# Rotation on VectorE a quad ahead, products of rounded activations first, roundings moved in the norm gaps, and the inverse's first turn placed earlier

## The reference, cut

```python
def _layer(x, pos, st, lp):
    h = _rmsnorm(x, lp['norm_mix_pre'])
    y, new_st = _token_mixers(h, pos, st, lp)     # 4 mLSTM, 4 retention, 8 gated-delta heads of 128
    x = x + _rmsnorm(y, lp['norm_mix_post'])
    h = _rmsnorm(x, lp['norm_mlp_pre'])
    u = jnp.square(jax.nn.relu(jnp.einsum('btd,df->btf', h, lp['w_up'])))      # 2048 -> 8192
    x = x + _rmsnorm(jnp.einsum('btf,fd->btd', u, lp['w_down']), lp['norm_mlp_post'])
    return x, new_st

def _rotary(x, pos):                              # q and k of the retention heads
    x1, x2 = x[..., :half], x[..., half:]
    return jnp.concatenate([x1 * cos - x2 * sin, x1 * sin + x2 * cos], axis=-1)
```

## Time and profile before

| | us |
|---|---|
| median of 3 runs | 3140.09 (3137.81 to 3142.33) |
| profiled execution | 3140.11 |
| its span, first to last instruction | 3138.6 |
| TensorE busy | 3054.0, 97% |
| VectorE busy | 1919.4, 61% |
| ScalarE busy | 1542.6, 49% |
| mean granted clock of TensorE | 0.994 |

### The profile page before, as it was taken

The page is one execution under the profiler, slowest core; times in us unless marked ns, Lnnn a source line. Parts: engine busy times, 40 slices in busy tenths (PEclk is TensorE's granted clock), DMA queues, the critical chain, the costliest instruction groups (busy, mean ns, idle before and its releaser), DMA issues.

```text
span 3138.6 us, 66992 instructions
## 1 busy us (share of the span) xinstructions
PE 3054.0 (97%) x23012; PEld 2985.0 (95%) x23012; DVE 1919.4 (61%) x3994; ACT 1542.6 (49%) x3580; POOL 85.6 (3%) x163
## 2 busy tenths in 40 slices
PE   8999999999999999999999999999999999999998
PEld 7999999998999999999989999999989999999997
DVE  6677776656545545455576777766565454554555
ACT  6476665545333334334455676655454333343343
POOL 1100000000000000000001000000000000000000
PEclk9999999999999999999999999999999999999999
DMA  6554445553544444444445444455535445444444
GB/s 210 178 153 138 140 140 157 168 180 127 170 165 161 165 162 167 161 162 166 155 142 177 146 145 143 138 163 159 171 129 167 160 163 167 165 162 166 163 164 155
DMA packets 267255, 499.96 MB, mean 159 GB/s; under 512 B 34528, under 2 KB 39936, under 8 KB 267072
## 3 DMA queue, kind: packets, MB, share of 16 engines
q1 hardware_dynamic: 244224, 443.64, 43.9%
q0 software_dynamic: 14784, 51.05, 4.7%
q10 hardware_dynamic: 8064, 2.80, 0.3%
HBM read 475.38 MB, written 22.01 MB: 158 GB/s over the span
## 4 chain that ended last, share of the span: by engine, by line
PE 80%; DVE 11%; ACT 5%; issue 3%; DMA 1%; ACTq 0%; DVEq 0%; POOL 0%; SPq 0%; POOLq 0%
PE PU L523 72%; PE PABCD L523 3%; DVE WL L1300 2%; PE PE_ L523 2%; PE PF L523 2%; ACT AE L899 1%; ACT Y L899 1%; DVE AE L1687 1%; ACT WH L899 1%; DMA RAW<-in_w 1%; DVE Y L1484 1%; DVE Y L1320 1%; DVE X L1327 0%; DVE HL L1305 0%; DVE AM L1592 0%
## 5 line engine op out<-in xcount | busy, mean ns | idle before, releaser
L523 PE MATMUL PU<-HH,WH 128*128 128x288 f32 x4000 | 1236.4, 309 | 29.5 <-DVE HL L1305 21.1
L899 ACT ACTIVATE WH<-RAW 128x512 fp32r<-128x512 f32 x1669 | 965.4, 621 | 583.4 <-PE PU L523 436.6
L1300 DVE TENSOR_TENSOR WL<-RAW,WH 128x512 fp32r<-128x512 f32 x1668 | 1077.1, 687 | 271.1 <-ACT WH L899 258.0
L523 PE MATMUL PU<-HL,WH 128*128 128x288 f32 x4000 | 1183.2, 296 | 0.0
L523 PE MATMUL PU<-HH,WL 128*128 128x288 f32 x4000 | 1180.2, 295 | 0.0
L523 PEld LDWEIGHTS PU<-HH,WH 128*128 128x128 f32 x4000 | 754.4, 189 | 61.1 <-issue 41.6
L523 PE MATMUL PU<-UH,WH 128*128 128x288 f32 x2560 | 759.1, 297 | 2.8 <-DVE UL L1475 1.9
L523 PEld LDWEIGHTS PU<-HL,WH 128*128 128x128 f32 x4000 | 755.9, 189 | 4.1
L523 PEld LDWEIGHTS PU<-HH,WL 128*128 128x128 f32 x4000 | 755.9, 189 | 0.0
L523 PE MATMUL PU<-UL,WH 128*128 128x288 f32 x2560 | 755.2, 295 | 0.0
L523 PE MATMUL PU<-UH,WL 128*128 128x288 f32 x2560 | 752.6, 294 | 0.0
(11 more groups left out here) (281 smaller groups left out, 2214.7 us busy)
## 6 DMA issues: line engine op xcount, KB each, us to landing
RAW<-in_w SPq DMA_DIRECT2D x1669, 256.0 KB, 3.8
SIN<-in_sin POOLq DMA_DIRECT2D x32, 512.0 KB, 4.9
out_sout<-Y POOLq DMA_DIRECT2D x32, 512.0 KB, 5.4
BC<-gate_rows POOLq DMA_DIRECT2D x32, 304.0 KB, 4.4
AUX<-in_aux POOLq DMA_DIRECT2D x32, 152.0 KB, 3.2
X<-in_x SPq DMA_DIRECT2D x4, 576.0 KB, 8.6
out_y<-X SPq DMA_DIRECT2D x8, 288.0 KB, 2.1
out_sout<-SOUT ACTq DMA_DIRECT2D x32, 64.0 KB, 2.4
```

The source lines that it names most:

```text
L523: return nc.tensor.matmul(out, lhsT, rhs, start=start, stop=stop, skip_group_check=True)
L899: return nc.scalar.activation(out, in_, f, **kw)
L1300: tt(WL[s % 2][:, k], RAW[c][:], WH[s % 2][:, k].bitcast(F32), ALU.subtract).then_inc(sem("lo_ready"), 1)
```

## The change

- **Rotation.** The two `c_rot` products and step 1's three VectorE instructions go. `rotate` does the same with four VectorE instructions in the quad ahead: z times cosine (128 rows), two halves of 64 rows of z times sine, each read from one half of the rows and written to the other, and the sum into QK2. They stand at slots 16, 17, 19 and 21 of the retention quads and at 19 to 22 of "first". Step 2 of a retention head moves from slot 8 to slot 6.
- **Order of products.** In quads with two units at once `pair_part` does, for each pair of chunks, the products with HH for both units (8 matmuls) in an even slot, waiting for `hh_ready`, and the products with HL (4 matmuls) in the odd slot behind it, waiting for `hl_ready`. Both units are done at slot 15.
- **Roundings in the gap.** `hi_part(Q, 4)` and `lo_part(Q, 4)` stand ahead of the norm's factor; pieces 5, 6 and 7 follow in groups 1, 3 and 5 on both engines. The last chunk's weighing by the gain (`weigh`) stands behind the factor.
- **Inverse.** XM is transposed at slot 3, ahead of NX, into Q2 and not XT.
- **Start.** The first gain is loaded by ScalarE's queue and not GpSimd's, and ScalarE rounds the first weights before it waits for it.

```diff
+RET_SLOTS = {**LINEAR_SLOTS, 2: 6}
+ROTATE_SLOTS, FIRST_ROTATE_SLOTS = (16, 17, 19, 21), (19, 20, 21, 22)
-SIDE_BY_SIDE = [(t % 2, t // 2) for t in range(16)] + [divmod(t, 8) for t in range(16, SLOTS)]
...
+            def pair_part(Q, t, kind, l):
+
+                kk, low = divmod(t, 2)
+                e = 2 * l + (1 if kind == "up_first" else 0)
+                if t == 0:
+                    pe.wait_ge(sem("psum_read"), 4 * Q + 2)
+                if not low and kk % 2 == 0:
+                    pe.wait_ge(sem("lo_ready"), 16 * Q + 4 + kk // 2 + 1)
+                for s in range(2):
+                    psum = PU[s][:, 0:T]
+                    for k in (2 * kk, 2 * kk + 1):
+                        if s == 0:
+                            pe.wait_ge(sem("hl_ready" if low else "hh_ready"), e * NC_ + k + 1)
+                        if low:
+                            last = mm(psum, WH[s][:, k], HL[:, k], False, k == NC_ - 1)
+                        else:
+                            mm(psum, WH[s][:, k], HH[:, k], k == 0, False)
+                            mm(psum, WL[s][:, k], HH[:, k], False, False)
+                    if t == 15:
+                        last.then_inc(sem("unit_done"), 1)
...
-                if step == 0 and not mls:
+                if step == 2:
                     pe.wait_ge(sem("z_ready"), 4 * n + 4)
-                    pe.wait_ge(sem("state_ready"), n + 1)
-                    mm(PC[:, 0:T], con["c_rot"][:], z[:, 0])
-                    mm(PD[:, 0:T], con["c_rot"][:], z[:, 1]).then_inc(sem("ret_rotated"), 1)
...
         def _(act):
+            act.dma_start(NG0[:], d["ng0"][0]).then_inc(sem("gain_at_start_in"), 16)
...
             def prenorm(l, e, gain, Q):
...
-                    if (e or l) and g in (0, 1, 3, 5):
-                        hi_part(Q, (g + 1) // 2 + 4)
+                    if (e or l) and g in (1, 3, 5):
+                        hi_part(Q, g // 2 + 5)
...
             def after_out(l):
+                Q = l * QUADS + HEADS + NC_ // 4
+                hi_part(Q, 4)
                 norm_scale(2 * l + 1, RS, "rs_ready")
-                prenorm(l, 2, NG[:, 1], l * QUADS + HEADS + NC_ // 4)
+                weigh(l, 0, NC_ - 1)
+                prenorm(l, 2, NG[:, 1], Q)
...
+            def rotate(t, nk, par, slots):
+
+                z, half = Z[par], HD // 2
+                cos, sin = con["c_cos"], con["c_sin"]
+                if t == slots[0]:
+                    dve.wait_ge(sem("constants_in"), 16 * len(con))
+                    tt(ACC[:, 0:2, 0:T], z[:, 0:2], cos[:].unsqueeze(1).to_broadcast([128, 2, T]), ALU.mult).then_inc(sem("ret_qk"), 1)
+                for j, (a, b) in ((1, (half, 0)), (2, (0, half))):
+                    if t == slots[j]:
+                        tt(EE[b:b + half, 0:2, 0:T], z[a:a + half, 0:2], sin[a:a + half].unsqueeze(1).to_broadcast([half, 2, T]), ALU.mult)\
+                            .then_inc(sem("ret_qk"), 1)
+                if t == slots[3]:
+                    dve.wait_ge(sem("ret_qk"), 4 * nk + 3)
+                    tt(QK2, ACC[:, 0:2, 0:T], EE[:, 0:2, 0:T], ALU.add).then_inc(sem("ret_qk"), 1)
...
                     dve.wait_ge(sem("gdn_root"), 2 * nk + 1)
+                    nc.vector.transpose(Q2, XM).then_inc(sem("gdn_root_turned"), 1)
                     tt(NX, EYES[:], XM, ALU.subtract).then_inc(sem("gdn_root"), 1)
...
-                if t == ROOT_SLOT:
-
-                    dve.wait_ge(sem("kv_turned"), n + 1)
-                    dve.wait_ge(sem("gdn_root"), 2 * nk + 1)
-                    nc.vector.transpose(XT, XM).then_inc(sem("gdn_root_turned"), 1)
...
             def update_and_split(l, which, lo_l, lo_which, lo_gain, Q):
 
+                lo_part(Q, 4)
                 for g in range(8):
                     scale_y(l, which, g)
                     if g != 1:
...
                     if g:
                         add_x(l, which, g)
                     if g in (1, 3, 5):
-                        lo_part(Q, g // 2 + 4)
+                        lo_part(Q, g // 2 + 5)
                 prenorm_lo(lo_l, lo_which, lo_gain, range(14, 16))
-                lo_part(Q, 7)
```

More of the change, by code:

```diff
@@ L526, in turn @@
                 return nc.tensor.transpose(out, in_, IDENT)
+            def pair_part(Q, t, kind, l):
[17 more added lines that the diff above has]
+                        last.then_inc(sem("unit_done"), 1)
             def unit_part(Q, t, kind, l, x, joined):
-                s, kk = JOINED[t] if joined else SIDE_BY_SIDE[t] if two_at_once(kind, l) else divmod(t, 8)
+                if two_at_once(kind, l) and t < 16:
+                    pair_part(Q, t, kind, l)
+                    return
+                s, kk = JOINED[t] if joined else divmod(t, 8)
                 hi, lo = (UH, UL) if kind in ("out", "down", "down0", "down_last") else (HH, HL)
@@ L644, in linear_head @@
                     pe.wait_ge(sem("head_done"), n + 1)
[L645 removed]
+                if step == 2:
                     pe.wait_ge(sem("z_ready"), 4 * n + 4)
[L647 to L654 removed]
+                    if not mls:
+                        pe.wait_ge(sem("ret_qk"), 4 * (nk + 1))
                     pe.wait_ge(sem("state_ready"), n + 1)
@@ L868, in mixer @@
                         linear_select(read_number(kind, l, x))
-                    for step, slot in (LAST_SLOTS if last else EARLY_SLOTS if early else LINEAR_SLOTS).items():
+                    for step, slot in (LAST_SLOTS if last else EARLY_SLOTS if early else RET_SLOTS if kind == "ret" else LINEAR_SLOTS).items():
                         if t == slot:
@@ L972, in output_squares, with weigh @@
                     act.wait_ge(sem("gains_in"), 16 * (l + 1))
-                gain = NG[:, 0 if kind == "out" else 2, c:c + 1]
-                fn(Y[:, c], Y[:, c], scale=gain).then_inc(sem("output_squares"), 1)
+                if c < NC_ - 1:
+                    weigh(l, 0 if kind == "out" else 2, c)
+            def weigh(l, which, c):
+                fn(Y[:, c], Y[:, c], scale=NG[:, which, c:c + 1]).then_inc(sem("output_squares"), 1)
             def norm_scale(count, dst, name):
@@ L1501, in linear_head @@
                             ts(CUR[:, :, j:j + 1], COLA[:, :, bass.ds(hk + r, 1)], 1.0, None, ALU.mult).then_inc(sem("mls_cur"), 1)
-                if step == 1 and not mls:
-                    tt(ACC[:, 0:2, 0:T], z[:, 0:2], con["c_cos"][:].unsqueeze(1).to_broadcast([128, 2, T]), ALU.mult)\
-                        .then_inc(sem("ret_qk"), 1)
-                    dve.wait_ge(sem("ret_rotated"), nk + 1)
-                    tt(EE[:, 0:2, 0:T], PABCD[:, 2:4, 0:T], con["c_sin"][:].unsqueeze(1).to_broadcast([128, 2, T]), ALU.mult)\
-                        .then_inc(sem("ret_qk"), 1)
-                    dve.wait_ge(sem("ret_qk"), 3 * nk + 2)
-                    tt(QK2, ACC[:, 0:2, 0:T], EE[:, 0:2, 0:T], ALU.add).then_inc(sem("ret_qk"), 1)
                 if step == 1 and mls:
@@ L1798, in quad @@
                         lo_part(Q, t // 2 + 4, l if last_head else None)
+                    if kind == "first":
+                        rotate(t, l * H_B, 0, FIRST_ROTATE_SLOTS)
+                    if kind == "ret" and not front:
+                        rotate(t, x[1] + 1, 1 - x[3], ROTATE_SLOTS)
                     if front:
```

34 lines of the change are left out of this document (17 added, 17 removed).

## The result

The changed kernel takes **3154.2 us** (median of 5 runs, 3153.0 to 3156.8) where the kernel before takes 3141.0 beside it: ratio **1.0044**, 95% interval 1.0033 to 1.0055, so 10 to 17 us slower. The forecast was 3145.1 us with a range up to 3154. The profiled span is 3153.6 us against 3138.6, which is 15.0 us more; the mean granted clock is 0.994 in both.

The account below looks back on a forecast made before the run. TensorE, busy 97% of the span, was taken as the bound, through its work and waits. 3140.1 - 8.8 (inverse) - 5.5 (rotation) + 19.3 (gaps with clock) = 3145.1 us, start 0; range 3134 to 3154 us.

Parts of the forecast that it names:

- The norm gaps: Three gaps with two units at once: VectorE's low parts stand for ScalarE's roundings, unit 2 loses cover; 16.9 us more.
- The clock: Ends of the norm gaps: one more stretch at half clock in one gap of three, 2.4 us more.
- Rival 1: Norm gaps' ends: waits bring the clock down at each, 7 us and not 2.4; 3150 us, chance 0.20.
- The inverse's turn: Delta heads: TensorE's wait at slot 6 goes, part returns at slot 7; 0.55 us a head, 8.8 us less.
- The rotation: Retention heads: two fp32 products leave TensorE in each of 8; 4.9 us gained, heads 0 lose 0.3 each; 5.5 us less.
- The start: Kernel start: ScalarE's earlier first rounding is lost again at the next; 0, ends 0.9 us gained and 0.4 us lost.
- The sum's second term: The rotation's gain in the retention heads, 5.5 us subtracted in the sum.
- the gaps at their upper end: Norm gaps, clock included: 19.3 us more was forecast, with ends 15 and 24.

Follow-up runs that it names:

- gap_early: The changed kernel with ScalarE rounding pieces 5, 6 and 7 in groups 0, 2 and 4 of the norm gaps, not 1, 3 and 5: 3134.0 us.
- old_order: As gap_early, but TensorE takes the products of two units at once in the order of the kernel before: 3130.8 us.
- rot_only: The kernel before with the rotation's part of the change alone (VectorE, quad ahead; step 2 in slot 6): 3146.2 us, ratio 1.0012.
- turn_only: The kernel before with only the inverse's transpose moved ahead of NX, its result into Q2: 3131.7 us, ratio 0.9968.
- gw_later: The changed kernel with GpSimd holding the gates' weights' two loads until the second quarter of X has landed: 3152.2 us, one execution.
- gap_state: As gap_early, with GpSimd holding the first head's states' load until the gates' reciprocal, not only the gates' projection: 3131.4 us.
- first_thin: The changed kernel with the first quads' four rotation instructions taking 32 of their 288 columns: 3153.2 us, ratio 1.0033.

## Why the prediction was wrong, step by step

**The norm gaps: right.** Three low parts stand 2.22 us each (2.35 foretold), and unit 2 has its wait of 1.31 us (1.4 foretold). The three gaps cost 5.7, 5.9 and 6.0 us (4.7, 6.6 and 5.6 foretold), together 17.6 us (16.9 foretold without the clock, 19.3 with it). gap_early shows that they hang on the stalls, and old_order that the lost cover costs more than the shorter tail gives.

**The clock: mis-sized.** I added 2.4 us for a stretch of half clock that the kernel before would not have had. Windows (columns as in the earlier trace rows) of the changed kernel at the end of its first gap, in layer 1's MLP gap and in the first retention head of layer 1, then of the kernel before and of rot_only in layer 1's MLP gap:

```profile
752.00:755.40 3.40, 3.40 (x16) 3.25 (x14) 1.47 (x3) 1.63 (x4) 0.00 (x0) 0.51 0.00 0
2314.00:2330.00 16.00, 11.08 (x69) 7.83 (x70) 10.65 (x21) 8.66 (x21) 0.00 (x0) 1.00 0.10 34
1629.10:1632.50 3.40, 3.40 (x16) 3.22 (x15) 0.92 (x4) 1.96 (x6) 0.00 (x0) 0.50 0.48 154
```
```profile
2314.00:2320.00 6.00, 6.00 (x43) 5.69 (x43) 3.97 (x7) 4.46 (x10) 0.00 (x0) 1.00 0.49 167
```
```profile
2314.00:2320.00 6.00, 5.25 (x30) 4.18 (x31) 1.61 (x4) 2.02 (x5) 0.00 (x0) 0.72 0.13 44
```

So the changed kernel ends its first gap at the 1.2 GHz level, as the kernel before did, and the last one at 2.4 GHz, again as before; in the first quad of layer 1 each of them has one such stretch. Rival 1 did not happen: the gaps' ends have no such stretch more than before, and of the 2.4 us nothing came. What one such stretch at a gap's end costs is seen in rot_only, whose gap is the old code: unit 2 starts 26.56 us behind the first scaling instead of 25.18, 1.4 us. The changed kernel has its extra one where I had none, in the first retention head of layer 1, right behind TensorE's wait of 1.87 us for the spread at 1628.79; the kernel before has no low stretch in its retention quads. It is a likely part of the +0.9 us there (layer 0: -0.2), and in gap_early the same head of layer 0 has one (from 57.9, behind a wait of 2.10 us).
The section that the prediction cites from the Trainium skill ("TensorE: Matmul & The Clock Gate", HAM oscillation) describes a kernel in which every burst of products starts low behind a wait for a transfer; those waits were longer than the ones here, and I carried the rule over without that. Here the traces have both, with the same code: behind equal waits in layer 1's MLP gap (1.96 us before, 1.97 in rot_only) the products ahead of unit 2 ran at a granted clock of 1.00 in the one and partly at the low level in the other (0.72 over the 6 us shown).

**The inverse's turn: right**, 0.61 us a head and 9.3 us in all for 8.8; turn_only gives the same by itself.

**The rotation: the step that failed.** I took a gain of 0.96 us for two and 0.75 us for four of the six heads that aren't a layer's first, and wrote that ScalarE's spread of k "is then just in time", with 0.2 us off in the four. It was late by 1.35 us a head on average (10.8 us in 8 heads, 2.4 us before), which is more than the 0.96 us that the products leave behind. The error was in what I counted for a moved step: I looked at TensorE's slot and at VectorE's QK2, and not at the queue of ScalarE between them, where the roundings of slots 1 and 3 stand for weights that have only just landed. The table gives +4.8 us where I had -5.5, a miss of 10.3 us where the whole one is 10.0 us; the other terms' misses cancel. Two runs put it at this step: with step 2 back in slot 8 the same quads stand at -4.2 us, and with the spread ahead of the rounding 12.5 us go. rot_only loses 3.4 us in its medians (0.9 to 6.6 by its interval) and 2.7 us at these places in its trace. The 2.1 us between that and 4.8 come up in layer 1 (the changed kernel loses 3.6 us there, rot_only 1.1), and for them the runs show two likely parts that they don't separate: the earlier projection, which let the states' load out, and the stretch of half clock. In head 0 of a layer I bounded the loss with 1 us; it was 1.4 us at unit 2's evacuation in layer 0 and 2.7 us in layer 1. What I had right there is that low parts come out late behind the rotation (a wait of 1.03 us for one at 52.76).

**The start: mis-sized.** I saw that the gate weights' loads move ahead and bounded the loss by 0.4 us; the second weights landed 9.4 us behind their issue and not 8.4, and 1.0 us was lost. gw_later shows that these loads were the cause.

**The 0.9 us in the mLSTM heads** of layer 0 stay open. Kernels with the same code there have it (gap_state, 0.9 us) or don't (first_thin and gap_early, below 0.1 us), so it comes and goes from one execution to the next. The two that have it show a wait of TensorE for VectorE's scores in the first of these heads (0.53 us at 555.24 in the changed kernel), and ahead of it a wait of ScalarE for weights of 3.85 and 4.00 us, against 3.21 before and 3.24 in first_thin; that the late weights are the cause is not shown.

**The range** ended 0.2 us short. The sum's second term had a lower end for heads 0 alone, and no case for the six others in which the rotation gives nothing. With that term at 0 the sum is 3150.6 us, and with the gaps at their upper end 3155 us: the case was to be had from the bounds that stood there already.

## What to carry to other kernels

When work that two engines hand to each other is reordered by one place in a loop, write down for each handoff which instruction of the producer now stands ahead of it; one place in the loop (1, 3, 5 instead of 0, 2, 4) cost 20 us here. A moved step is as early as the slowest in-order queue that feeds it, and an instruction in that queue that waits for a transfer counts with its wait, not with its length. And a transfer that was held by a slow engine starts early when that engine gets faster: look up what it then travels beside.

## What the runs showed of the hardware

A 64-row instruction of VectorE takes as long as one of 128 rows. First quad of layer 1, gap_early:

```profile
1596.69 0.75 DVE L1603 TENSOR_TENSOR AE<-Z,c_cos 128x576 f32<-128x576 f32 x1
1597.47 0.75 DVE L1606 TENSOR_TENSOR AE<-Z,c_sin 64x576 f32<-64x576 f32 x1
1598.25 0.69 DVE L1325 TENSOR_TENSOR WL<-RAW,WH 128x512 fp32r<-128x512 f32 x1
```

So halving the rows saved nothing (0.75 us each), and the distance from start to start is 0.78 us, where two instructions of 128 rows overlap and have 0.67 us (from the sum at 54.28, to the next instruction at 54.95). The Trainium skill ("VectorE: DVE Perf Modes", Two Vector instructions with no wait between them) says that an instruction is held until its forerunners have finished when its input or output starts in another group of 32 partitions than the last one did; the traces agree, with 0.1 us each.

A transfer makes another one in flight visibly longer: the second weights, issued at 2.38 us in all three kernels, landed 8.4 us behind their issue when the first of the gates' two loads (512 KB each) went out at 2.21 us, 9.4 us when it went out at 1.53 us, and 7.4 us when it waited until 8.99 us (gw_later). The Trainium skill ("DMA: Bandwidth & Descriptors", Queues, rings and completion order) has the DMA engines go round their queues packet by packet, which would fit; no run here shows the turns themselves.
